# Expert weights in a one-core encoder layer: raw gate and up halves laid out row by row instead of one after the other

## What is computed

```python
x = layer_norm(ALPHA * x + token_mixer(x), ...)
x = layer_norm(ALPHA * x + cross_attend(x, mk, mv, w_xq, w_xo), ...)
x = layer_norm(ALPHA * x + hier_moe(x), ...)

def hier_moe(x, lp):          # top 1 of 4 groups, then top 2 of the 8 experts in it
    ...
    def expert_block(args):
        e, toks, wts = args
        xb = xt[toks]                                   # (rows, 1024)
        h = silu(xb @ w_g[e]) * (xb @ w_u[e])           # w_g, w_u: (1024, 512)
        return (h @ w_d[e]) * wts[:, None]              # w_d: (512, 1024)
```

## Time and profile before

| | |
|---|---|
| device time, median of 3 runs | 1674.16 us (1672.81 to 1675.77) |
| profiled execution | 1672.81 us, its span 1671.0 us |
| PE busy | 1596.4 us, 96% of the span |
| DVE, ACT busy | 998.7 us (60%), 764.7 us (46%) |
| granted TensorE clock over the span | 0.98 |
| DMA | 351.91 MB, mean 211 GB/s |
| expert stage | about 1035 to 1610 us |

### The profile page before, as it was taken

One profiled execution on the slowest core, in us unless ns is written; L12 is line 12 of the kernel. 1 busy time (PEld: TensorE's weight loads), 2 busy tenths in 40 slices (PEclk: granted clock), 3 DMA queues, 4 the chain that ended last, 5 costly groups with the idle time before them and its releaser, 6 DMA issues.

```text
span 1671.0 us, 21261 instructions
## 1 busy us (share of the span) xinstructions
PE 1596.4 (96%) x8282; PEld 1286.0 (77%) x8282; DVE 998.7 (60%) x1359; ACT 764.7 (46%) x1070; POOL 244.5 (15%) x210
## 2 busy tenths in 40 slices
PE   8999999999998999999999988999999999999956
PEld 4678887577776788999877767788888888888842
DVE  1420111477756457222445447999999899999936
ACT  2311111333335102222422222888888888888834
POOL 0000000000007381000022111111111111111005
PEclk9999999999999999999999987999999999999988
DMA  9610111700011554300235545899999999999867
GB/s 356 242 54 31 68 55 59 239 21 21 12 64 51 202 177 169 122 26 14 101 130 174 188 166 194 318 388 393 388 398 390 379 393 398 393 391 389 323 255 295
DMA packets 85152, 351.91 MB, mean 211 GB/s; under 512 B 24498, under 2 KB 27186, under 8 KB 63172
## 3 DMA queue, kind: packets, MB, share of 16 engines
q1 hardware_dynamic: 74932, 330.69, 52.4%
q0 software_dynamic: 9216, 18.89, 2.9%
q10 hardware_dynamic: 912, 1.05, 0.2%
HBM read 322.19 MB, written 43.15 MB: 219 GB/s over the span
## 4 chain that ended last, share of the span: by engine, by line
PE 92%; ACT 3%; DVE 2%; DMA 1%; issue 1%; POOL 0%; SPq 0%; DVEq 0%; POOLq 0%; ACTq 0%
PE M L1219 32%; PE M L948 12%; PE T L767 6%; PE M L758 5%; PE T L701 4%; PE T L822 4%; PE M L833 4%; PE T L1260 3%; PE M L701 2%; PE T L1022 2%; PE T L1020 2%; PE T L1021 2%; PE M L1054 2%; PE M L725 2%; PE M L1036 2%; PE T L1314 2%
## 5 line engine op out<-in xcount | busy, mean ns | idle before, releaser
L1219 PE MATMUL M<-rounded 128*128 128x512 f32 x2304 | 543.1, 394 | 7.2 <-DVE rounded L1696 2.8
L1696 DVE TENSOR_TENSOR rounded<-beside,rounded 128x1024 fp32r<-128x1024 f32 (+2 forms) x394 | 473.5, 1237 | 91.3 <-ACT rounded L1329 47.3
L1219 PEld LDWEIGHTS M<-rounded 128*128 128x128 f32 x2304 | 429.3, 189 | 95.6 <-issue 4.9
L1584 ACT CAST rounded<-beside 128x1024 fp32r<-128x1024 f32 x256 | 263.0, 1050 | 63.0 <-DMA beside<-in_w_exp_up 33.9
L948 PE MATMUL M<-rounded 128*128 128x512 f32 x864 | 210.2, 398 | 2.9 <-ACT rounded L1454 1.6
L948 PEld LDWEIGHTS M<-rounded 128*128 128x128 f32 x864 | 160.8, 190 | 36.3 <-issue 2.2
L1594 ACT CAST rounded<-beside 128x1024 fp32r<-128x1024 f32 x128 | 131.3, 1052 | 26.1 <-PE M L1219 17.3
L1696 DVE TENSOR_TENSOR rounded<-T,rounded 128x512 fp32r<-128x512 f32 (+1 forms) x82 | 81.7, 1000 | 26.5 <-ACT rounded L1467 17.7
L1407 ACT ACTIVATE arena<-T,negmax 128x384 f32<-128x384 f32 (+3 forms) x64 | 47.3, 740 | 102.0 <-DVE negmax L1771 102.0
L701 PE MATMUL T<-tables,arena 128*128 128x128 f32 x572 | 80.0, 284 | 14.6 <-DMA arena<-in_mem_prompt 6.5
L701 PEld LDWEIGHTS T<-tables,arena 128*128 128x128 f32 x572 | 68.7, 146 | 31.1 <-issue 9.6
(11 more groups left out here) (311 smaller groups left out, 2115.3 us busy)
## 6 DMA issues: line engine op xcount, KB each, us to landing
beside<-in_w_exp_gate SPq DMA_DIRECT2D x64, 1024.0 KB, 7.9
beside<-in_w_exp_up SPq DMA_DIRECT2D x64, 1024.0 KB, 10.6
beside<-in_w_exp_down SPq DMA_DIRECT2D x32, 2048.0 KB, 10.9
arena<-x_rows SPq DMA_DIRECT2D x27, 512.0 KB, 3.6
x_rows<-arena SPq DMA_DIRECT2D x18, 512.0 KB, 3.1
arena<-expert_rows SPq DMA_DIRECT2D x9, 1024.0 KB, 12.6
arena<-in_x_prompt SPq DMA_DIRECT2D x16, 512.0 KB, 4.2
arena<-in_cache_mem_k SPq DMA_DIRECT2D x8, 1024.0 KB, 5.7
```

The source lines that it names most:

```text
L1219: got = nc.tensor.matmul(out, x[xs], (high, low)[ws](w)[:, c:c + 512], start=(first and n == 0), stop=(last and n == 2))
L1584: nc.scalar.copy(as_both(high(c)), both_raw(c)).then_inc(gu_high, 1)
L1696: return nc.vector.tensor_tensor(out, x, highs.bitcast(f32), ALU.subtract)
```

## The change

The two DMAs of a half now write the rows of gate and up interleaved: row k of gate goes to columns 0 to 511 of row k of the buffer, row k of up to columns 512 to 1023. Each DMA then has 4 pieces of 2 KB per partition instead of one of 8 KB, at the destination 4 KB apart. A chunk lies in one run of 1024, so ACT and DVE read it as such, and the helpers `both_raw` and `as_both` go. For down the text of the DMA is another, its shape when built is the same (128x4096). Sizes, order, waits and semaphores stay. The lines behind the definitions move up by eight, in part by seven.

```diff
--- before.py
+++ after.py
@@ -256,15 +256,7 @@
         mk_b, mv_b, mkT_b = area(40192, 2, D), area(42240, 2, D), area(44288, KT, MEM)
 
         CH = 12
-        w_raw = [beside[:, o:o + 4 * D] for o in (0, 8448, 12544)]
-        gate_raw, up_raw = ([w_raw[g][:, at:at + 4 * FE] for g in (0, 1)] for at in (0, 4 * FE))
-        down_raw = w_raw[2].rearrange("p (k n) -> p k n", k=4)
-
-        def both_raw(c):
-            return w_raw[c // 4].rearrange("p (s k n) -> p k s n", s=2, k=4)[:, c % 4, :, :]
-
-        def as_both(part):
-            return part.rearrange("p (s n) -> p s n", s=2)
+        w_raw = [beside[:, o:o + 4 * D].rearrange("p (k n) -> p k n", k=4) for o in (0, 8448, 12544)]
 
         def halves(at, n):
             return [[rounded[:, at + (2 * u + s) * n:at + (2 * u + s + 1) * n] for s in (0, 1)] for u in (0, 1)]
@@ -635,8 +627,9 @@
                     load_x1(t + 1)
 
             def load_half(e, g):
-                for src, raw in ((w_gate, gate_raw), (w_up, up_raw)):
-                    sp.dma_start(raw[g], src[ds(e, 1), :, 4 * g:4 * g + 4, :].rearrange("e p k n -> p (e k n)")).then_inc(raw_in[g], 16)
+                for src, c in ((w_gate, 0), (w_up, FE)):
+                    sp.dma_start(w_raw[g][:, :, c:c + FE],
+                                 src[ds(e, 1), :, 4 * g:4 * g + 4, :].rearrange("e p k n -> p (e k) n")).then_inc(raw_in[g], 16)
 
             sp.wait_ge(o_low, 4)
             load_half(0, 0)
@@ -647,7 +640,7 @@
             store_x2(PT)
 
             def load_down(e):
-                sp.dma_start(w_raw[2], w_down[ds(e, 1), :, :, :].rearrange("e p k n -> p (e k n)")).then_inc(raw_in[2], 16)
+                sp.dma_start(w_raw[2], w_down[ds(e, 1), :, :, :].rearrange("e p k n -> p (e k) n")).then_inc(raw_in[2], 16)
 
             load_down(0)
             for b in range(NE):
@@ -1581,7 +1574,7 @@
                         act.wait_ge(w_used, 2 * KT + c + 1)
                     else:
                         act.wait_ge(gu_used, 8 * b - 8 + c + 1)
-                    nc.scalar.copy(as_both(high(c)), both_raw(c)).then_inc(gu_high, 1)
+                    nc.scalar.copy(high(c), w_raw[c // 4][:, c % 4, :]).then_inc(gu_high, 1)
 
             def split_down(b, chunks):
                 for c in chunks:
@@ -1591,7 +1584,7 @@
                         act.wait_ge(w_used, 3 * KT)
                     else:
                         act.wait_ge(down_used, 4 * b - 4 + c + 1)
-                    nc.scalar.copy(high(8 + c), down_raw[:, c, :]).then_inc(down_high, 1)
+                    nc.scalar.copy(high(8 + c), w_raw[2][:, c, :]).then_inc(down_high, 1)
 
             def softmax(n, tiles):
                 act.wait_ge(softmax_in, 3 * n + 1)
@@ -1971,12 +1964,12 @@
             def split_gate_up(b, chunks):
                 for c in chunks:
                     dve.wait_ge(gu_high, 8 * b + c + 1)
-                    take_low(as_both(low(c)), both_raw(c), as_both(high(c))).then_inc(gu_low, 1)
+                    take_low(low(c), w_raw[c // 4][:, c % 4, :], high(c)).then_inc(gu_low, 1)
 
             def split_down(b, chunks):
                 for c in chunks:
                     dve.wait_ge(down_high, 4 * b + c + 1)
-                    take_low(low(8 + c), down_raw[:, c, :], high(8 + c)).then_inc(down_low, 1)
+                    take_low(low(8 + c), w_raw[2][:, c, :], high(8 + c)).then_inc(down_low, 1)
 
             for t in range(NT):
                 u = t % 2
```

## The result

The changed kernel takes 1683.45 us (median of 8 runs, 1678.87 to 1686.58) beside 1673.31 us for the kernel before (median of 8 runs on the same chip): ratio 1.0052, 95% interval 1.0039 to 1.0065. By the medians it is slower by 10.1 us, where 19.5 had been forecast. The ratio is taken over more runs, 26 of the changed kernel with a median of 1681.37 us; by the ratio the loss is 8.7 us. The profiled execution took 1681.36 us, its span 1679.4.

What follows compares the result with a forecast made beforehand. PE bound the expert stage at 17.77 us a turn, DMA close behind at 17.4; pieces add 1.04, so DMA leads by 0.70: 21 us over 30 turns, less 1.5, is 19.5, forecast 1693.5 us; range 1678 to 1706 for 8 in 10.

Steps and rivals of the forecast that it cites:

- Two limits lie close, and the loads pass PE: Expert stage: PE's turn 17.77 us sets the pace; after the change the DMA's 18.47 us does, 0.70 over.
- The DMA's turn of 17.4, reserve 0.35 us: Expert stage before the change: 6.88 MB a turn at 395 GB/s take 17.4 us, 0.35 under PE's 17.77.
- 4.19 MB take 9.82 us at 427 and 10.87 us at 386: 1.04 us more a turn: Gate and up loads: price of 2 KB instead of 8 KB pieces, from rates of two other loads, 1.04 us a turn.
- in the stage the 8 KB pieces don't reach 427 but 395 GB/s, for a reason that the rows don't show. If that reason also hides what pieces cost: Lower bound in the expert stage: 2 KB pieces cost only 0.25 us a turn, 17.65, under PE's turn, so no change.
- The path: Expert stage: late half 1 of the next expert delays chunks 5 and 6, silu and product, then PE's gate and up.
- The 1.5 us that are absorbed once: First full turn of the stage: product done at 1071.26, needed at 1072.74, so 1.5 us of lateness cost nothing.
- Reading as one run, worth nothing: ACT and DVE chunk reads: one run of 1024 instead of two of 512 gains nothing; ACT 1050 against 1052 ns.
- Holding SP: SP issuing loads: may be held longer by more queued pieces; a load of 1024 2 KB pieces held the next DMA 5.14 us.
- Hidden pieces: Rival 1, stage loads: full-rate sum gives the changed kernel a 17.2 us turn, under 17.77; no change, 1674 us; chance 0.15.
- Clock: Rival 2, expert stage: PE's gaps lower its clock; at 0.9 it costs 36 us more, 1730 us; chance 0.03.
- Faster: Rival 3, gathered rows before their transposes: land earlier behind 2 KB pieces; at most 7.2 us gained, 1670 us; chance 0.04.
- Not in smaller pieces: Rival 4, gate and up loads: source is one 8 KB run, so nothing changes; counted in rival 1, no chance of its own.

Runs made afterwards that it cites:

- the runs with two products: Third matmul of each split product left out in the expert stage: kernel before (8 KB pieces) 1668.01 us, ratio 0.9968; changed kernel (2 KB) 1682.71 us, 1.0055.
- The loads alone: Kernel with only the weight loads, eight experts per piece size: an expert takes 14.84 us with 8 KB, 15.13 with 4, 15.74 with 2, 16.97 with 1.
- 24 us of gaps: Changed kernel with gate and up landing in 1 KB pieces, 8 per partition and DMA: 1705.25 us, ratio 1.0191.
- engine traffic: Only the weight loads, beside DVE, ACT, PE or all three working on other tiles: 14.84 us an expert throughout, 15.72 with 2 KB pieces and all three.
- spread rows in the stage: Third matmul of each product left out, each expert's rows spread over the partitions: changed kernel 1662.51 us, ratio 0.9924; kernel before 1652.26 us, 0.9862.
- held buffers: Only the weight loads, each buffer held some 6 us after landing: 15.66 us an expert over all six steps with 8 KB pieces, 16.13 with 2 KB.
- unbalanced rows: Only the weight loads, beside gathers and scatters of 72 rows in the first 72 partitions: 17.80 us an expert with both, 18.03 with 2 KB pieces.
- beside spread rows: Only the weight loads, beside gathers and scatters of 72 rows spread over partitions: 16.44 us an expert with both, 17.29 with 2 KB pieces.
- silu's place: Silu and the hidden product put ahead of chunks 5 and 6 of the next expert: changed kernel 1684.23 us, ratio 1.0054; kernel before 1674.65 us, 0.9996.

## Why the prediction was half right

- **Two limits lie close, and the loads pass PE: right.** Shown by the runs with two products, where PE waits 101 and 107 us for the product and ACT 97 and 110 us for landings: their turns are 17.63 and 18.1 to 18.4 us, on either side of PE's 17.77.
- **The DMA's turn of 17.4, reserve 0.35 us: mis-sized.** Measured 17.63 and 0.14. The term was bytes by the rate of one stretch of 89 us at share 1.00, 395 GB/s; over 450 us in which PE didn't hold them back the loads moved 392. Alone, this would have added 0.21 us a turn, 6.3 us. It pulls against the next error: with the reserve right and the price left at 1.04, the forecast would have been 25.8 us, so by luck it came out nearer.
- **"4.19 MB take 9.82 us at 427 and 10.87 us at 386: 1.04 us more a turn": the step that failed.** The loads alone pay 0.90, so the rates of rows 6 were near. The forecast took it that the stage pays the same; in the stage 0.49 are paid, 16.5 us less over 30 turns. The bound "in the stage the 8 KB pieces don't reach 427 but 395 GB/s, for a reason that the rows don't show. If that reason also hides what pieces cost" had named it, and the forecast passed it over.
- **The sum with measured terms:** 0.49 - 0.14 = 0.35 us a turn, 10.5 over 30 turns, less 1.5 absorbed: 9.0 us, beside 10.1 measured in the medians, 8.7 by the ratio and 8.6 in the profiled executions. The interval of the 0.49 makes it 5.4 to 12.6 us, so that they agree is worth no more than that.
- **The path: right,** The earlier trace rows and the turn at 1361.51: half 1, silu, product, PE. PE waits on no low part in the stage. The 1.5 us that are absorbed once fit too: four turns still take 17.77 us, at 0.35 us each 1.4 us. "Then each turn pays in full" does not: turns at PE's pace lie between the late ones, and only their mean is 0.35 us longer. Its idle time was put at some 25 us and is 12.3, smaller with the loss and partly hidden in busy time.
- **Reading as one run, worth nothing: right.** 1049 and 1047 ns beside 1050 and 1052. **Holding SP,** for which the sum has no term: rightly, an up issue in the stage took SP 0.51 us in the median and 1.67 at most, before the change 0.43 and 1.05.
- **Packets:** 85152 before, 134303 after, 49,151 more, one short of 1536 x 32; between 1060 and 1585 us 44,300 more, where 46,000 had been said. GB/s fell to 381, not 372, and a turn to 18.07, not 18.3 to 18.7.
- **The rivals.** Hidden pieces: no, though true of half their price. Clock: 1.00, and still 1.00 with 24 us of gaps. Faster: no, PE waits for no gathered rows in the stage, before or after. Not in smaller pieces: no, by the packets. The Trainium skill, "DMA: Bandwidth & Descriptors", section Specifications, by which transfers from 512 B up run at line rate, does not agree with these runs: 2 KB pieces lose 0.49 us in the stage and 0.90 of 15.74 in the loads alone. The overhead of some 3 cycles a packet in the same page's section "Why small descriptors are slow (HBM only)", 3.5% of gate and up as the prediction estimated from it, is less than the 9% that the loads alone show.

What makes the price smaller in the stage is narrowed but not settled. It isn't engine traffic (0.88 with all of them), nor the imbalance by itself (0.34 with spread rows in the stage). It is smaller wherever something else also delays a load: 0.15 to 0.47 us with held buffers, 0.23 beside unbalanced rows, 0.63 with both. The packets' own records in the traces (1100 to 1550 us in the kernels) say which pieces differ. A piece of 2 KB takes a mean of 87 to 90 ns in all these kernels. A piece of 8 KB takes 314 ns in the loads alone, 312 beside spread rows, but 327 with held buffers, 338 beside unbalanced rows and 328 in the stage before the change. The 14 ns between the stage and the loads alone are 0.45 us over the 32 pieces of a turn and engine, about what the price in the stage lacks of the price alone (0.90 less 0.49). So a reading is that the long pieces were already slowed in the stage before the change, and that short ones aren't slowed in the same way. It doesn't account for all: in the stage with rows spread 8 KB pieces take 317 ns and the price is still only 0.34. Why the long pieces are slowed, no run isolates. Whether silu's place has any worth beside late loads is open too.

## What to carry to other kernels

A busy share of 1.00 on the DMA engines says neither that they are used fully nor evenly: a share of 0.99 to 1.02 went with 384 and with 424 GB/s. Where two limits lie within 2%, measure the one behind by taking work from the one ahead, before pricing an edit; and don't charge the price that a transfer pays alone to a stage that already runs below the rate it has alone. Small pieces cost this kernel nothing once the DMA had been given room, here by spreading partly filled gathers and scatters over the partitions.

## What the runs showed of the hardware

- In loads that have the DMA to themselves a piece costs 9.1 to 9.5 ns of an engine's time on top of its bytes, between 8 KB and 1 KB: 425, 417, 399, 371 GB/s.
- A piece of 8 KB took a mean of 314 ns alone and 327 to 338 ns where buffers were held or rows fell unevenly; a piece of 2 KB took 87 to 90 ns in all of these.
- An indirect gather or scatter of 72 rows of 4 KB in the first 72 partitions costs the loads beside it 1.25 or 1.45 us; spread over the partitions, 0.8. In the stage spreading is worth 0.5 to 0.7 us a turn.
- PE, DVE and ACT at the stage's rates change nothing in the DMA's (425 and 423 GB/s).
- PE's clock stayed at 1.00 with 24 us of idle time over 525 us, and its mean was 0.90 where it was idle for a fifth of the time (two products, 8 KB).
